# Expert weights of the projection stage split in pieces of 512 columns with four buffers, instead of 1024 with two

## The reference, cut to what matters

```python
h = rmsnorm(x, ln1_g)
proj = h @ w_in                                  # 1024 -> 3080 columns
xc, new_conv_l = causal_conv(x_lru, conv_l, lru_cw)
hs, new_h = rglru(xc + lru_cb, h_l, ...)         # gates, then a scan over time
out_a = hs * gelu(y_lru)
qkv_c = silu(causal_conv(qkv, conv_g, gdn_cw))
o, new_S = gdn_sequence(S, q, k, v, g, beta)
x = x + concat(out_a, rmsnorm(o) * silu(z)) @ w_out
x = x + hier_moe(rmsnorm(x, ln2_g), ...)         # 32 experts, top 2 of a group:
                                                 # (silu(xb @ w1[e]) * (xb @ w3[e])) @ w2[e]
y = rmsnorm(x, final_g)
```

## Time and profile before

| | |
|---|---|
| median of 3 runs | 4324.17 us (4323.01 to 4324.24) |
| the profiled execution | 4329.62 us, span of its instructions 4328.0 us |
| TensorE busy in the span | 3577.7 us (83%) |
| VectorE busy | 2200.0 us (51%) |
| ScalarE busy | 1679.3 us (39%) |
| GpSimd busy | 947.6 us (22%) |
| mean granted TensorE clock | 0.927 of 2.4 GHz |

### The profile page before, as it was taken

One profiled execution on the slowest core, in us unless ns is written; L12 is line 12 of the kernel. 1 busy time (PEld: TensorE's weight loads), 2 busy tenths in 40 slices (PEclk: granted clock), 3 DMA queues, 4 the chain that ended last, 5 costly groups with the idle time before them and its releaser, 6 DMA issues. The chain is left out here.

```text
span 4328.0 us, 72419 instructions
## 1 busy us (share of the span) xinstructions
PE 3577.7 (83%) x21028; PEld 2176.8 (50%) x21029; DVE 2200.0 (51%) x4880; ACT 1679.3 (39%) x2974; POOL 947.6 (22%) x1046
## 2 busy tenths in 40 slices
PE   8987696886978589899989999998739999999920
PEld 3443343333434567666766766676524444444410
DVE  6566474664756445655655565556432222222257
ACT  6556465564655433333333333333112222222222
POOL 0000000000000123333333334333111111111145
PEclk9998898998989699999999999999869999999965
DMA  4465656656565312121112111221046666774379
GB/s 146 150 207 195 223 191 216 213 198 212 196 202 190 131 35 68 53 65 58 63 53 65 58 63 54 64 68 54 15 185 225 224 231 220 271 269 151 107 293 381
DMA packets 293079, 656.24 MB, mean 152 GB/s; under 512 B 26467, under 2 KB 138595, under 8 KB 292579
## 3 DMA queue, kind: packets, MB, share of 16 engines
q1 hardware_dynamic: 182162, 321.70, 23.4%
q0 software_dynamic: 56512, 186.76, 11.5%
q10 hardware_dynamic: 54288, 146.56, 8.7%
HBM read 404.57 MB, written 250.38 MB: 151 GB/s over the span
## 5 line engine op out<-in xcount | busy, mean ns | idle before, releaser
L341 PE MATMUL pP<-h_hi,w_hi 128*128 128x512 f16 (+1 forms) x1728 | 634.8, 371 | 59.4 <-ACT win L435 40.1
L341 PE MATMUL pP<-h_lo,w_hi 128*128 128x512 f16 (+1 forms) x1728 | 634.6, 371 | 0.0
L341 PE MATMUL pP<-h_hi,w_lo 128*128 128x512 f16 (+1 forms) x1728 | 632.8, 370 | 0.0
L1631 PE MATMUL ebank<-ws_sb,rowsT 128*128 x2352 | 528.3, 382 | 40.0 <-issue 39.0
L1631 PEld LDWEIGHTS ebank<-ws_sb,rowsT 128*128 128x128 f16 x2352 | 229.4, 98 | 313.7 <-issue 67.6
L542 DVE SCALAR_TENSOR_TENSOR halves<-stage,halves 128x1024 f16<-128x1024 f32 x192 | 234.5, 1222 | 248.5 <-ACT halves L411 248.5
L293 POOL DMA_DIRECT2D ws<-halves x192 | 103.2, 537 | 1122.1 <-DVE halves L542 615.8
L577 DVE SCALAR_TENSOR_TENSOR cv<-win,cols_sb,cv 128x512 f32<-128x512 f32 (+1 forms) x432 | 305.5, 707 | 33.9 <-issue 0.9
L1247 DVE TENSOR_TENSOR WI<-bank,const 128x512 f32<-128x512 f32 x198 | 136.5, 690 | 351.6 <-PE bank L919 347.1
L341 PEld LDWEIGHTS pP<-h_hi,w_hi 128*128 128x128 f16 x1728 | 174.3, 101 | 256.2 <-ACT win L435 44.6
L411 ACT ACTIVATE halves<-stage 128x1024 f16<-128x1024 f32 x192 | 201.9, 1052 | 259.8 <-POOLq L296 255.7
(11 more groups left out here) (290 smaller groups left out, 6036.3 us busy)
## 6 DMA issues: line engine op xcount, KB each, us to landing
stage<-in_we SPq DMA_DIRECT2D x192, 512.0 KB, 4.1
ws<-halves POOLq DMA_DIRECT2D x192, 512.0 KB, 3.9
ws_sb<-ws SPq DMA_DIRECT2D x32, 3072.0 KB, 13.7
y<-yb ACTq DMA_DIRECT2D x98, 512.0 KB, 4.7
ft<-mixin SPq DMA_DIRECT2D x33, 1280.0 KB, 6.1
mixin<-qo ACTq DMA_DIRECT2D x128, 256.0 KB, 2.8
xt<-in_x SPq DMA_DIRECT2D x33, 512.0 KB, 5.9
xr<-in_x SPq DMA_DIRECT2D x33, 512.0 KB, 4.8
```

The costliest lines, as they stand in the source:

```text
L341: ins = nc.tensor.matmul(pP[n % NPB][:, 0:N], w[:, k, c0:c0 + P], h[:, k, 0:N], start=(k + i == 0), stop=(k == KD - 1 and i == 2))
L1631: ins = nc.tensor.matmul((M0, M1)[p][:, :], xT[p][:, x, k, :], half(s, k // 2, w, k % 2 * 512), start=(k + i == 0), stop=(k == KD - 1 and ...
```

## The change

The constant `WC` goes from 1024 to 512, so that there are 384 W steps with half the columns each (12 an expert); `stage` and `halves` keep their size and are cut in four buffers of 512 columns (`WS`). Semaphores of the loads and of the stores are one for each buffer. ScalarE's wait for `halves_free` begins with 4 instead of 2; SyncE may load step q when VectorE is done with step q-4.

A group has 56 W steps (48 in group 7). They are dealt out in `sequence()`: 2 after each Y and X, 3 after each of Q0 to Q3, 2 after each of Q4 to Q11, 4 after each of Z0, Z1 and Z2, none after Z3.

On GpSimd `halved(q)` now waits for VectorE's step q, issues the store of q, and only then waits for the landing of the store of step q-2 and increments `halves_free` for it (`stored`). The first group of the loop is written out.

In the expert stage `half()` takes the index of a 512-column piece; the matmuls and their operands stay the same. The loads of an expert move the same 3 MB in rows of 2 KB instead of 4 KB, as do the W steps.

```diff
-WC = 1024
+WC = 512
-NW = 28
+NW = 56
+WS = 4
@@ sequence()
-            for _ in range(2 if kind == "Z" else 1):
+            for _ in range({"Z": (4, 4, 4, 0), "Q": (3,) * 4 + (2,) * 8}.get(kind, (2,) * 4)[m]):
@@ project_phase()
+        stage4 = stage[:, :, :, :].rearrange("p s k n -> p (s k n)").rearrange("p (s n) -> p s n", s=WS)
-        halves = sb("halves", [P, 2, 2, WC], FP16)
+        halves = sb("halves", [P, WS, 2, WC], FP16)
-        expert_in = [sem(f"expert_in{n}") for n in range(2)]
+        expert_in = [sem(f"expert_in{n}") for n in range(WS)]
-        halves_out = sem("halves_out")
+        halves_out = [sem(f"halves_out{n}") for n in range(WS)]
@@ sync
-                    sp.dma_start(stage[:, j % 2, :, :].rearrange("p k n -> p (k n)"),
-                                 T["we"][bass.ds(q, 1)].rearrange("a p n -> p (a n)")).then_inc(expert_in[j % 2], 16)
+                    sp.dma_start(stage4[:, j % WS, :],
+                                 T["we"][bass.ds(q, 1)].rearrange("a p n -> p (a n)")).then_inc(expert_in[j % WS], 16)
@@ gpsimd
+            def stored(q, j):
+                pool.wait_ge(halves_out[j % WS], (q - j % WS) * (16 // WS) + 16)
+                pool.sem_inc(halves_free, 1)
+
             def halved(g, j):
                 q = (g - 1) * NW + j
-                pool.wait_ge(expert_lo, q + 3)
+                pool.wait_ge(expert_lo, q + 1 + WS)
                 pool.dma_start(T["ws"][bass.ds(q, 1)].rearrange("a p n -> p (a n)"),
-                               halves[:, j % 2, :, :].rearrange("p h n -> p (h n)")).then_inc(halves_out, 16)
-                pool.wait_ge(halves_out, 16 * q + 16)
-                pool.sem_inc(halves_free, 1)
+                               halves[:, j % WS, :, :].rearrange("p h n -> p (h n)")).then_inc(halves_out[j % WS], 16)
+                if not isinstance(q, int) or q >= 2:
+                    stored(q - 2, j - 2)
@@
-            with pool.Fori(1, groups - 1) as g:
+            stores(1, GT)
+            with pool.Fori(2, groups - 1) as g:
                 stores(g, GT)
             stores(groups - 1, 1)
+            for q in (NC - 2, NC - 1):
+                stored(q, q)
@@ scalar
-                    act.wait_ge(expert_in[j % 2], ((g - 1) * (NW // 2) + j // 2 + 1) * 16)
+                    act.wait_ge(expert_in[j % WS], ((g - 1) * (NW // WS) + j // WS + 1) * 16)
                     act.wait_ge(halves_free, q + 1)
-                    nc.scalar.activation(halves[:, j % 2, 0, :], stage[:, j % 2, :, :].rearrange("p k n -> p (k n)"),
+                    nc.scalar.activation(halves[:, j % WS, 0, :], stage4[:, j % WS, :],
                                          ACT.Copy, scale=W_SCALE).then_inc(expert_hi, 1)
-            act.sem_inc(halves_free, 2)
+            act.sem_inc(halves_free, WS)
@@ vector
-            dve.sem_inc(expert_lo, 2)
+            dve.sem_inc(expert_lo, WS)
-                    nc.vector.scalar_tensor_tensor(halves[:, j % 2, 1, :], stage[:, j % 2, :, :].rearrange("p k n -> p (k n)"),
-                                                   W_SCALE, halves[:, j % 2, 0, :], ALU.mult, ALU.subtract
+                    nc.vector.scalar_tensor_tensor(halves[:, j % WS, 1, :], stage4[:, j % WS, :],
+                                                   W_SCALE, halves[:, j % WS, 0, :], ALU.mult, ALU.subtract
@@ experts_phase()
-        def half(s, c, h, off):
+        def half(s, c, h):
-            return ws[:, bass.ds(s, 1), c, h * WC + off:h * WC + off + 512].rearrange("p a n -> p (a n)")
+            return ws[:, bass.ds(s, 1), c, h * WC:(h + 1) * WC].rearrange("p a n -> p (a n)")
```

More of the change, by code:

```diff
@@ L1630, in step @@
                         for i, (x, w) in enumerate(PARTS):
-                            ins = nc.tensor.matmul((M0, M1)[p][:, :], xT[p][:, x, k, :], half(s, k // 2, w, k % 2 * 512),
+                            ins = nc.tensor.matmul((M0, M1)[p][:, :], xT[p][:, x, k, :], half(s, k, w),
                                                    start=(k + i == 0), stop=(k == KD - 1 and i == 2))
@@ L1649, in step @@
                             ins = nc.tensor.matmul((OA, OB)[h][:, :], guT[p][:, x, k, :],
-                                                   half(pe_slot[0], W13 // WC + k, w, h * 512),
+                                                   half(pe_slot[0], W13 // WC + 2 * k + h, w),
                                                    start=(k + i == 0), stop=(k == FE // P - 1 and i == 2))
```

## The result

The changed kernel takes 4408.0 us (median of 4 runs, 4404.62 to 4414.03), the kernel before 4324.2 beside it: a ratio of 1.0194, 95% interval 1.0176 to 1.0212. The forecast had the side right (slower), but its range ended at 4384. The profiled execution has a span of 4403.1 us, 75.1 more than before, where the forecast had 21 more; the medians lie 83.8 us apart. What follows is read from the two profiled executions and so accounts for the 75.1.

A forecast was written before the change was run, and what follows sets the result against it. Projection groups were held bounded by ScalarE's pace from Q0 to Q3 and store waits at their end. Six groups at +2 us and group 7 at +9 gave +21: 4351 profiled, 4345 median; own range 4322 to 4372, overall 4296 to 4384.

The forecast's parts named there:

- The tail: End of a projection group: eight W steps of 4.4 us become twelve pieces of about 1.4, gaining 16 us.
- the mixing stage: Stage after the projection: nothing changes there.
- The third piece: After Q0 to Q3, ScalarE's third copy waits for the same chunk's first piece: +5.8, +5.8, +6.9 us for Q0 to Q2.
- the block: ScalarE held from Q0 to Q3: costs 18 us a group, 15 to 21 held possible.
- The norm: VectorE's norm in mid-group, where it waits 9.10 us for GpSimd: moves 18 us later.
- The chain: Tail: copy, rest, issue, landing and release take 1.19 to 1.39 us a piece, 14.3 to 16.6 for twelve.
- The transfer bound: Tail: 6.3 MB at 343 GB/s take 18.4 us, plus 1.3 for copy and rest: +3.3 us a group.
- Group 7: Last projection group, with 48 steps: first `h_lo` of group 8 comes 9 us later, between +5 and +18.
- The weighed rule: Tail: at 425 GB/s the 6.3 MB take 14.8 us and the whole is 12 us less; the row's 343 was used.
- The third piece doesn't wait: Rival, Q0 to Q3: buffers are free, only the tail's gain is left, -16 us a group, 4220 us; chance 0.12.
- a smaller block: Rival, Q0 to Q3: existing waits absorb part, 12 us a group instead of 18, 4303 us; chance 0.10.
- Transfers: Rival, tail: the last 20 us get only 261 GB/s, +9 us a group, +63 in all, 4387 us; chance 0.16.

The follow-up runs named there:

- two pieces each: Changed kernel with two pieces after every Y, X and Q chunk and four after each Z, Z3 included: 4310.2 us, ratio to before 0.9971.
- the one with more in front: Changed kernel with four pieces behind each of Y0, X0, Y1, X1 and two behind every other chunk: 4268.0 us, ratio 0.9868; with 56 drains 4231.9 us.

## Why the prediction was right or wrong

Two steps of the forecast failed. The tail was to gain 16 us a group and gained 12.3. And the mixing stage, held at nothing, is 12.2 us longer in the profiled execution, from loop turns that cost 20.6 us more. Of the 54 us by which the measured 75.1 exceed the forecast's 21, the five full groups from 2 to 6 make 36, the mixing stage 12.2, group 1 3.8, the start 3.2, and group 7 -0.7. The further 8.7 us between the medians lie in no trace; how much of them is the scatter ahead of the turns isn't shown.

- **The third piece.** Right. Waits of 5.07, 5.08, 6.21 and 3.68 us, "some 5" in the forecast; the squares of the norm 18.6 us later against 18. TensorE's wait for evictions is 128.3 us, over 120 as said. With two pieces each the block has gone but for 2.4 us.
- **The norm.** A term was missing, worth 1.3 us. The forecast moved it as it was. GpSimd's gap grew by 2.3 us, of which 1.3 are left, since it no longer waits for a landing ahead of it: 19.9 us for the scaling.
- **The tail.** The failed step of the projection, and the largest: 12.3 us gained instead of 16, so 3.7 in each of six groups. Twelve pieces took 1.83 us each ((536.83 - 514.87) / 12), not 1.2 to 1.6, and both bounds were too low. The chain was reckoned with landings of 2.8 to 3.6 us; they took 4.45 on the mean, which gives (0.62 + 0.69 + 0.64 + 4.45) / 4 = 1.6 us a piece, and GpSimd, which waits for a landing before it issues the next store, adds to that: 43 of the 72 stores start within 0.9 us of the landing of the store three before. The transfer bound had 24 transfers and 6.3 MB at a full share. From 514.87 to 536.83 the trace has 26 (13 stores, 9 loads, 4 silus) and 6.8 MB, 311 GB/s at a share of 0.91. That is 343 at a full share, the same as read before, so the rate was right; the count was short, and the share stayed under 1. Last, where two bounds stood side by side, I took a value between them (+2 and not +3.3), though the later one had to decide. TensorE's wait before the transposes therefore fell to 99.5 us, not to 60.
- **The turn of the group.** Held at nothing, it cost 1.5 us: with no piece behind Z3 its eviction and store stand between ScalarE's last copy and the first `h_hi`; with pieces behind Z3 it is 2.3 to 3.0 us instead of 4.4. The half clock stayed, as forecast: the granted clock is 0.5 of 2.4 GHz from 528.84 to 545.91 us, where it was 0.5 from 500.84 to 528.14 before.
- **Groups.** So a full group is 9.2 us longer instead of 2: 7.2 for five of them, and 3.8 for group 1. Group 7 is 8.3 us longer against +9, by the path that was named: before the first `h_lo` of group 8 ScalarE's eviction of Z3 waits 1.26 us for TensorE. That the value between +5 and +18 was hit so closely is luck.
- **The mixing stage.** "Nothing changes" was the other step that failed: 20.6 us more in loop turns, though its code is the same. With 56 idle instructions more in VectorE's program the same kernel is 44 us faster, so the place of the loop is the cause; the packets of the q14 instruction queue went from 85 to 161 over the kernel. Of the 12.2 us net, the 10.8 gained ahead of the turns are scatter and 2.4 were lost behind them; without that luck this miss would be some 20 us. The expert stage cost nothing, as said.
- **Start.** 3.2 us come before group 1. Kernels with the same code there begin it between 166.7 and 170.2 us, so this is no more than scatter.
- **A slip without effect.** Nine rests, not eight, lie in the 35.4 us from 485.70 to 521.08; the eight behind Q11's own take 34.2, so 4.3 each. And the 18.4 us that the sum holds for twelve pieces are 1.5 each, not 1.4. The sum goes by the end times and doesn't use either.
- **The weighed rule.** The Trainium skill, HBM Reference, section Specifications (TRN2), gives some 425 GB/s to a core alone. The tail moved 316 at a share of 0.92, so 343 at a full one, as before; for the tail the measurement decides. But that no run shows 425 is not right: in the combination stage of the kernel before, with reads and writes mixed, 418 GB/s flow from 4176 to 4226 us, at a full share. So the Trainium skill's figure nearly holds in this case, and what keeps the tail below it is open.
- **The rivals.** "The third piece doesn't wait" and "a smaller block" are out. "Transfers" came nearest in the total, 4387, but not by its mechanism: it had 6.3 MB at 261 GB/s, 24.1 us and 1.3 for copy and rest; the trace has 6.8 MB at 311 in 22.0 us. The rest up to 4408 is the mixing stage and the norm.

## What to carry to other kernels

A resource that is released two items behind must not be asked for three times between two points at which the releasing engine waits: count the items per stretch, not the buffers. Where a tail is bounded by a chain and by bytes, count every transfer in it, take the landings as long as they are under that load, and take the later bound. Compare a stage over several runs before a gain or loss of some us in it is called an effect. And an edit that lengthens an engine's program moves all loops behind it: compare the instruction queue's packets and the idle times without a releaser at the start of a loop turn, and try a pad of idle instructions before a stage is called slower for a reason of its own.

## What was not expected of the hardware

- A loop of the same code costs 94.0 to 97.0 us a turn depending on where it stands in VectorE's program, and two pairs of kernels that differ by 256 instructions have the same turns; 56 instructions that do nothing gained 44 us in the changed kernel, 36 in the one with more in front, and 21 in the kernel before.
- A store of 256 KB landed no sooner than one of 512 KB (4.0 us against 3.9 over the whole kernel), and sooner (3.5 instead of 4.1 us in a tail) when other traffic was less.
- In GpSimd's loop the gap between two dependent operations of the norm is 4.80 us, 2.6 to 3.9 in the copy of the same code ahead of the loop and 4.7 to 6.0 in that behind it, with stores under way or without.
- The granted clock of the first 50 us of the mixing stage scatters between 0.58 and 0.88 over kernels with the same code there, and the stretch ahead of the turns between 194 and 183 us with it.
